# A third 512-column product per shared attention unit, and SyncE's last gate store and first V block issued from the experts' program

## The reference, cut to what matters

```python
def one(args):                                  # attention, 8 heads, blocks of 128 queries
    qn, qr = args
    s = jnp.einsum('bqhd,bkhd->bhqk', qn, k_nope) + jnp.einsum('bqhd,bkd->bhqk', qr, k_rope)
    p = jax.nn.softmax(s.astype(jnp.float32) * scale, axis=-1).astype(v.dtype)
    return jnp.einsum('bhqk,bkhd->bqhd', p, v)
...
g = jax.nn.softmax(sc.astype(jnp.float32), axis=-1).astype(xt.dtype)
act = jax.nn.gelu(jnp.einsum('thkd,td->thk', jnp.take(u_tab, eidx, axis=0), xt))
return jnp.einsum('thk,thkd->td', g * act, jnp.take(v_tab, eidx, axis=0))
```

## Time and profile before

| | |
|---|---|
| median of 3 runs | 3856.0 us (3841.12 to 3856.24) |
| the profiled execution | 3853.9 us |
| its span | 3851.8 us |
| PE / DVE / POOL / ACT busy | 92% / 89% / 51% / 37% of the span |
| HBM read / written | 977.45 / 53.56 MB |

### The profile page before, as it was taken

One profiled execution on the slowest core, in us unless ns is written; L12 is line 12 of the kernel. 1 busy time (PEld: TensorE's weight loads), 2 busy tenths in 40 slices (PEclk: granted clock), 3 DMA queues, 4 the chain that ended last, 5 costly groups with the idle time before them and its releaser, 6 DMA issues. The chain is left out here.

```text
span 3851.8 us, 60773 instructions
## 1 busy us (share of the span) xinstructions
PE 3547.2 (92%) x20332; PEld 3196.1 (83%) x20352; DVE 3419.5 (89%) x7139; ACT 1416.3 (37%) x2495; POOL 1958.6 (51%) x1568
## 2 busy tenths in 40 slices
PE   4989999589999999999978999958899999999997
PEld 4957799469999999999978678957789999999996
DVE  8975769988999999999989666799799999999998
ACT  3332332473333333333333223317533333333333
POOL 1000123586677677777610002227767777777774
PEclk9988999799999999999989889989999999999998
DMA  6720101259999999999957001103699999999997
GB/s 243 235 72 24 63 23 40 83 215 408 405 405 405 405 395 407 406 405 405 374 181 231 26 1 63 45 18 153 280 405 405 405 405 405 395 406 405 405 405 275
DMA packets 308141, 1033.75 MB, mean 268 GB/s; under 512 B 31354, under 2 KB 83386, under 8 KB 301314
## 3 DMA queue, kind: packets, MB, share of 16 engines
q0 software_dynamic: 147456, 536.94, 35.4%
q1 hardware_dynamic: 160514, 494.71, 33.9%
HBM read 977.45 MB, written 53.56 MB: 268 GB/s over the span
## 5 line engine op out<-in xcount | busy, mean ns | idle before, releaser
L1687 POOL DMA_INDIRECT picked_rows<-in_v_rows,chosen x512 | 801.8, 1566 | 260.4 <-DVE y L2022 141.9
L1687 POOL DMA_INDIRECT picked_rows<-in_u_rows,chosen x512 | 743.2, 1452 | 330.8 <-DVE dots_now L2014 213.3
L1893 PE MATMUL ps<-hd_hi,u_hi 128*128 128x384 f32 x2048 | 698.0, 341 | 1.3 <-DVE a_lo L2004 1.3
L1893 PE MATMUL ps<-hd_hi,u_lo 128*128 128x384 f32 x2048 | 694.1, 339 | 0.0
L1893 PE MATMUL ps<-hd_lo,u_hi 128*128 128x384 f32 x2048 | 693.2, 338 | 0.0
L2022 DVE SCALAR_TENSOR_TENSOR y<-picked_rows,dots_now,y 128x1024 f32<-128x1024 f32 x512 | 643.6, 1277 | 0.1
L2014 DVE CUSTOM_DVE_ANT_0 picked_rows<-picked_rows,h2rows 128x1024 f32<-128x1024 f32 x512 | 615.3, 1216 | 18.5 <-DMA picked_rows<-in_u_rows,chosen 17.0
L1904 PE MATMUL ps<-v_hi,a_lo 128*128 128x512 f32 x1536 | 474.5, 390 | 0.0
L1904 PE MATMUL ps<-v_hi,a_hi 128*128 128x512 f32 x1536 | 473.3, 389 | 0.0
L1904 PE MATMUL ps<-v_lo,a_hi 128*128 128x512 f32 x1536 | 472.9, 389 | 0.0
L1227 POOL TENSOR_TENSOR wout_lo<-wout_even,wout_hi 128x2048 fp32r<-128x2048 f32 x4 | 18.3, 4577 | 773.8 <-ACT wout_hi L1128 773.8
(11 more groups left out here) (324 smaller groups left out, 7133.4 us busy)
## 6 DMA issues: line engine op xcount, KB each, us to landing
u_raw<-in_u SPq DMA_DIRECT2D x256, 512.0 KB, 14.3
v_rest<-in_v SPq DMA_DIRECT2D x192, 512.0 KB, 8.0
mod_ring<-in_ada SPq DMA_DIRECT2D x96, 512.0 KB, 4.4
gt<-gates_dram SPq DMA_DIRECT2D x60, 768.0 KB, 15.4
gates_dram<-gmat SPq DMA_DIRECT2D x10, 4096.0 KB, 11.5
v_first<-in_v SPq DMA_DIRECT2D x64, 512.0 KB, 12.5
wq<-in_wq SPq DMA_DIRECT2D x32, 512.0 KB, 3.5
w_odd<-in_w_in SPq DMA_DIRECT2D x8, 1024.0 KB, 4.9
```

The lines of the kernel that those rows point to most:

```text
L1687: pool.indirect_dma_start(picked_rows[:, n % RING, :], None, a[table], bass.IndirectOffsetOnAxis(ap=chosen[:, m % GT, m // GT:m // GT + 1] ...
L1893: ins = pe.matmul(ps[:, b % 2, 0:TD], (u_hi, u_lo)[wl][:, b % 2, k, :], (hd_hi, hd_lo)[hl][:, k, :], start=(k == 0 and n == 0), stop=(k == ...
```

## The change

In `attend(n)`, for the 15 shared units, a product of 512 columns (`ident_b` and `maskb`, 16-bit) into the unit's own output bank is added behind the waits and ahead of the real products, which start their accumulation afresh. It follows the two of `filler()` as a third per unit.

In `gate_matrices`, SyncE now issues only the first half of the first gates (L1706 and L1709 for q = 0) after the last evacuation wait, without the wait for `staged`, and ends. The rest goes out from SyncE's program of `experts`, in the order: V block 0, store of rows 32 to 80, the second half of the first gates, wait for `g_part`, V blocks 1 to 3, stores of rows 0 to 32 and 80 to 128, wait for `gm_stored[1]`. `g_own` becomes two semaphores; DVE waits for the first before its loop and for the second at block 4 of each body.

```diff
@@ -883,6 +883,8 @@
                         pe.wait_ge(o_taken, n if n <= SHARED else n - 1)
+                    if n < SHARED:
+                        pe.matmul(ps[:, out_bank(n), :], ident_b[:, :], maskb[:, 0, :], start=True, stop=True)
                     tiles = keys(t)[2]
@@ -1687,6 +1689,13 @@
+    def first_gates(sp, q):
+
+        sp.dma_start(gt[:, q, 0:NB - 1, :, :].rearrange("p b k t -> p b (k t)"),
+                     gates_dram[0:NB - 1, :, 4 * q * GB:4 * (q + 1) * GB].rearrange("b p n -> p b n")
+                     ).then_inc(g_in[q], 16)
+        sp.dma_start(gt[:, q, NB - 1, :, :], gmat[:, 0, 4 * q:4 * q + 4, :]).then_inc(g_own[q], 16)
@@ -1700,17 +1709,7 @@
                         sp.wait_ge(gm_stored[0], 16 * turns + 16)
-                        sp.wait_ge(staged, turns + 1)
-                        for q in range(2):
-                            blocks = slice(4 * q, 4 * q + 4)
-                            sp.dma_start(gt[:, q, 0:NB - 1, :, :].rearrange("p b k t -> p b (k t)"),
-                                         gates_dram[0:NB - 1, :, 4 * q * GB:4 * (q + 1) * GB].rearrange("b p n -> p b n")
-                                         ).then_inc(g_in[q], 16)
-                            sp.dma_start(gt[:, q, NB - 1, :, :], gmat[:, 0, blocks, :]).then_inc(g_own, 16)
-                        sp.dma_start(v_first[:, :], a["v"][l, 0]).then_inc(v_in[0], 16)
-                        for (lo, hi), done in (((32, 80), g_part), ((0, 32), gm_stored[1]), ((80, NKEYS), gm_stored[1])):
-                            sp.dma_start(gates_dram[NB - 1, :, lo * GB:hi * GB],
-                                         gmat[:, 0, lo:hi, :].rearrange("p a b -> p (a b)")).then_inc(done, 16)
+                        first_gates(sp, 0)
                         return
@@ -1867,9 +1866,17 @@
+                def last_gates(lo, hi):
+                    return sp.dma_start(gates_dram[NB - 1, :, lo * GB:hi * GB], gmat[:, 0, lo:hi, :].rearrange("p a b -> p (a b)"))
+
+                load_v(0, 0)
+                last_gates(32, 80).then_inc(g_part, 16)
+                first_gates(sp, 1)
                 sp.wait_ge(g_part, 16)
                 for b in range(1, 4):
                     load_v(0, b)
+                last_gates(0, 32).then_inc(gm_stored[1], 16)
+                last_gates(80, NKEYS).then_inc(gm_stored[1], 16)
                 sp.wait_ge(gm_stored[1], 16 * (NB // 2) + 32)
@@ -1991,10 +1998,12 @@
-                dve.wait_ge(g_own, 32)
+                dve.wait_ge(g_own[0], 16)
...
+                    if b == 4:
+                        dve.wait_ge(g_own[1], 16)
```

More of the change, by code:

```diff
@@ L1680, in build_program @@
     gm_stored = [K.sem(f"gm_stored{i}") for i in range(2)]
-    g_own = K.sem("g_own")
+    g_own = [K.sem(f"g_own{i}") for i in range(2)]
     g_part = K.sem("g_part")
```

## The result

| | before | after |
|---|---|---|
| median, 4 runs each | 3852.1 us (3841.12 to 3856.24) | 3888.06 us (3881.01 to 3900.34) |
| the profiled execution / its span | 3853.9 / 3851.8 us | 3900.34 / 3898.2 us |

The ratio is 1.0093, 95% interval 1.0067 to 1.012: the change makes the kernel slower by 0.9%, some 36 us. The forecast was 3871, a loss of 15.6 us, with 3888 as the top of its range: the median lies on that edge, and the loss is more than twice the forecast one. "Before" is the three runs known ahead of the prediction and a fourth, 3848.19. One execution of `e4_gathers_later` took 13368 us, in a slow state, and is in its median but not in its ratio.

A forecast was written before the change was run, and what follows sets the result against it. TensorE was taken to pace the experts and attention, with the transfers full too. Experts +16.6 and attention -1.0 gave +15.6 us on 3853.9, so 3869.5; the median lies 2.1 above: 3871, range 3842 to 3888.

The forecast's parts named there:

- TensorE's 13 us of standing: Experts, before hidden(4): TensorE would stand idle some 13 us, from about 886.3 until 899.
- the 0.32 us steps after it: Experts, after the stall before hidden(4): products would start 0.32 us apart, against 0.18 when warm.
- the small stalls of blocks 4 to 10: Experts: these blocks would find their data ready, returning 0.8 us in layer 0 and 1.6 in layer 1.
- Part 1: End of the gate program: with SyncE no longer last, the experts start 6.0 and 6.1 us earlier.
- the change doesn't do what it says: Boundary: SyncE not last any more, no earlier start; counted near the forecast, without a chance of its own.
- Part 2: Experts' start: U 4, issued only after all stores land, makes hidden(4) 7 us later, bounds 0 and 11.
- Part 3: Experts: TensorE's restart at low clock after a 13 us stall costs 2.5 us per layer, between 0 and 3.5.
- Part 4: Shared attention units: third product costs 6.5 us, the clock gives 7.5 back: -1.0, bounds -16.2 to +11.6.
- the fall read in the earlier trace: Attention, unit pair from 307.31: clock fell just after the new product's place; the product may prevent that fall.
- D: Slower beyond doubt: part 2 as forecast, no clock back in attention, further falls: +28.2 us, 3884, chance 0.12.
- A: Experts: bytes are conserved, U 4 may land at 888.5 although issued later; 3858, chance 0.22.
- B: The change pays in full: U 4 in time, 6.0 and 6.1 us gained at the boundary; 3840, chance 0.12.

The follow-up runs named there:

- e4_gathers_later: Kernel before with POOL's first four gathers moved from the end of the gate program to the experts' program: 3863.67 us, ratio 1.0009.
- the two-gather kernel: Kernel before with first gates and first V block loaded before the last evacuation, two of POOL's four gathers moved to the experts' program: 3841.85 us.

## Why the prediction was right and wrong

**What it got right.** Slower, by the store order and the stall ahead of hidden(4); TensorE's 13 us of standing (13.53 measured); the 0.32 us steps after it; the return of the small stalls of blocks 4 to 10 (excess before 0.8 and 1.5 us, none there after); the steady part untouched.

**Part 1, the boundary: the step that failed.** "SyncE is the last to leave" was read from one coincidence, SyncE's last issue ending 3.4 us before ACT's first. Of POOL it said that its fourth gather "ends beside" TensorE, which counts the issue and not the landing. The lines on the end of the program show POOL as last, in both kernels. The 3.4 us were no cost of leaving either: where SyncE is really last, with the gathers moved, the same distance is 0.6 us (849.06 to 849.69). So of the 6.0 and 6.1 us that the experts should have started earlier, 0.8 and 1.0 came. The case "the change doesn't do what it says" was named and wrongly priced as near the forecast: without the earlier start hidden(4) is not 7 but 13 us later, and the forecast's own terms then give 2 x 7 + 6.0 + 6.1 + 2 x 2.5 - 2.4 = 28.7 for the experts. They lost 26.1.

**Part 2, the stores: right in kind, short by 3 us, and partly for another reason.** Relative to the program's start, U 4 was forecast at 31.9 us and issued at 34.9; V 1 to 3 were issued in time (11.3 against 11.9), and their bytes and the 2560 KB behind them were nearly all moved by 900, 29.5 us after V 0, forecast 29.9. The term that was too small is the one for a store's landing being seen after its last bytes, 2 us with 4 as its upper end: for 5.4 us, 900 to 905.4, SyncE's queue moved only 0.11 MB more, beside 2.13 MB of gathers, and the wait went on. What held these last 0.11 MB among the gathers is not shown. U 4 was in use 5.3 us after its issue, not 6.0. From the last evacuation, hidden(4) came at 42.0 us before and at 55.1 after, 13.0 later; forecast 7, plus 5.2 for the missing start, plus 3.0, less 0.7 of landing, 0.9 between ACT's and TensorE's steps (2.9 us instead of 3.8) and 0.5 of rounding. The term named only the order. The runs with the stores first and with the wait moved show two more shares: the first store, issued 5.1 and 4.1 us later than before, and V 0, 8.3 and 5.1 us later, leave the transfers dry (1.8 MB not moved, 4.4 us), and the wait itself is worth 4 to 7 us of length. The forecast had the store go out "nearly as before" and V 0 3 us later. How they add within the 14 us can't be told exactly, since each of these runs turned another block's data late.

**Part 3, the clock.** +2.5 forecast for the restart; the excess of 15.55 us less the 13.53 of standing leaves 2.0.

**Part 4, the product: the sum was near, both its terms were off.** It costs 1.6 to 1.9 us per layer at like clock, 3 to 4 together, and not 6.5; and nothing shows the 7.5 us that the clock should give back: 0.81 and 0.84 after, against 0.85 and 0.87 before over the same stretch, and a spread of 0.75 to 0.94 without the product. The forecast's -1.0 became +3 to +4. The reasoning "not under a wait as the two of filler() are" was the wrong way round: a product in the filler pays 3.0 of its 3.2 us, the one of the change about half. And the fall read in the earlier trace rows was one draw of something that differs from run to run; one execution was no basis for a gift of 7.5 us.

**The sum.** Experts 26.1 for 16.6, attention 3 to 4 for -1.0: about 30, with the medians 36 apart and the ratio's interval from 26 to 46 us. That the median falls on the top of the stated range owes nothing to the account: that top stood above D for an unknown landing, and what filled the distance was, for the larger part, the missing start.

**The rivals.** A (conserved bytes, 3858) lost on this change. The reason that the text gave against it, SyncE's queue empty while it waits for the stores, did happen, from 900 to 905.4; but the engines did not stand still, gathers filled them, and the bytes that were lost were lost at the boundary. Its mechanism is not dead: in the kernel before, taking 1.8 MB out of the full stretch gave about 3 to 4 us per layer. B did not come about: U 4 came late, and the start it needed was not there. D's 3884 is near the measured time and its mechanism is not what happened; the agreement is chance. What was missing was a rival in which another engine held the boundary.

## What to carry to other kernels

Before pricing an earlier exit of one engine, read the DRAIN and event lines of every engine's queue at the program's end: POOL's lasts until its own gathers have landed, long after the last issue. Where the transfers are full behind a boundary, shortening it may gain nothing by itself, above all if the loads needed first are issued later for it; look for a stretch in which they are idle ahead of it, move loads there, and only then free the boundary. A store put behind the loads of one queue is not out of the way: the next load stands behind it, with or without a wait. And one profile of a stage whose clock wanders is no basis for a price.

## What the runs showed of the hardware

- POOL's DRAIN at the end of a program: 13.8 to 15.0 us with four gathers of 512 KB issued at its end in the kernels before and after (11.1 and 16.1 with the loads early), 10.5 to 10.8 with two, 2.9 to 3.5 with none. It ended 0.2 us after the fourth gather had landed (before and after, both layers). SyncE's, with 4 MB of stores under way, 0.1 us. SyncE's queue does not wait for its transfers there, POOL's does.
- Gathers moved 220 GB/s nearly alone and 105 beside SyncE's stores, which had 328 in the same 6 us. The last 0.11 MB of SyncE's stores took 5.4 us while gathers moved 2.13 MB (after, layer 0); in layer 1 SyncE's queue moved 0.07 MB and the gathers 1.59 in the last 4 us ahead of U 4.
- TensorE's clock after a gap: idle 9.50 us at the boundary, the next products came 0.32 us apart (1.2 GHz). Idle 2.93 us with the gathers moved, layer 0, they came 0.18 apart at once and the stretches from 845 to 860 stand at 1.00; in layer 1 of the same execution, idle only 2.63 us, the clock fell 2.0 us into the gap and the eight warming products took 2.90 us, as after 9.50. The idle time alone does not tell whether the clock falls. After 3.94 us in the two-gather kernel, layer 1, the eight warming products still ran at full speed (1.86 us) and the products behind them came 0.32 apart: the fall came after the gap.

```profile
849.80 1.63 PE L1917 MATMUL ps<-hd_hi 128*128 128x384 f32 x8 [2.93 <-PEq L1694]
...
2754.07 2.90 PE L1917 MATMUL ps<-hd_hi 128*128 128x384 f32 x8 [2.63 <-PEq L1694]
```

- The granted clock of one and the same stage, with the same instructions, was 0.75 in layer 0 and 0.94 in layer 1 of one execution, 102.0 against 82.8 us. Differences of a few us between two single profiles of that stage mean nothing unless the clock is taken out.
